# Side work of a two-layer trunk kernel: slices used in fours, B0/E0 in another tile, and the S5 tap matrices loaded early in pieces of 16 partitions

## The reference

```
x = x_prompt   (and again for x_sample, which reads cached context and starts from a given state)
for l in 0, 1:
    sh_m, sc_m, g_m, sh_f, sc_f, g_f = split(silu(c) @ ada_w[l] + ada_b[l], 6)          # "adaLN parts"
    h = x * (1 + sc_m) + sh_m
    out = [windowed attention | latent attention](h)     if l == 0
    out = s5_mixer(h)                                     if l == 1
    x = layer_norm(alpha * x + g_m * out)
    h = x * (1 + sc_f) + sh_f
    x = layer_norm(alpha * x + g_f * moe(h))              # 64 experts, top 6, and a shared one

s5_mixer: u = h @ w_in_c
          y = C (scan of lam_bar * state + b_bar u), forward and backward, + d * u
          z = gelu(y) @ w_out_c;  result z_val * sigmoid(z_gate)
moe:      sum over experts of gate_e * (silu(t @ w_gate_e) * (t @ w_up_e)) @ w_down_e
```

## Time and profile before

| what | value |
|---|---|
| median of three runs | 1595.81 us |
| the profiled execution | 1592.51 us |
| its span | 1590.7 us (1.8 us lie around it) |
| TensorE matmul busy | 1424.2 us, 90% of the span |
| VectorE busy | 1042.0 us, 66% |
| ScalarE busy | 582.7 us, 37% |
| DMA, mean over the span | 234 GB/s |

### The profile page before, as it was taken

The page is one execution under the profiler, slowest core; times in us unless marked ns, Lnnn a source line. Parts: engine busy times, 40 slices in busy tenths (PEclk is TensorE's granted clock), DMA queues, the critical chain, the costliest instruction groups (busy, mean ns, idle before and its releaser), DMA issues. The chain is left out here.

```text
span 1590.7 us, 26708 instructions
## 1 busy us (share of the span) xinstructions
PE 1424.2 (90%) x10938; PEld 1299.7 (82%) x10938; DVE 1042.0 (66%) x1542; ACT 582.7 (37%) x680; POOL 35.1 (2%) x37
## 2 busy tenths in 40 slices
PE   4887699999999999999955559599999999999996
PEld 1866688989988899899955559499999999999995
DVE  7534487788778888788861543866555655655655
ACT  2434253333333333333321553443343333333332
POOL 2000100000000000000020000100000000000001
PEclk8979889999999999999968779799999999999998
DMA  9763388999999888887767585265556555555530
GB/s 364 281 224 110 142 282 288 326 335 330 316 323 330 335 290 276 300 277 247 258 208 190 143 299 212 74 231 213 195 192 213 198 191 214 201 188 212 203 141 27
DMA packets 144688, 372.96 MB, mean 234 GB/s; under 512 B 16760, under 2 KB 63192, under 8 KB 141600
## 3 DMA queue, kind: packets, MB, share of 16 engines
q1 hardware_dynamic: 144608, 371.87, 68.2%
HBM read 349.21 MB, written 21.50 MB: 233 GB/s over the span
## 5 line engine op out<-in xcount | busy, mean ns | idle before, releaser
L271 PE MATMUL PS<-moe_mod_HThl,moe_up_h 128*128 128x256 f32 x2080 | 592.5, 285 | 2.3 <-DVE moe_up_l L1613 2.3
L272 PE MATMUL PS<-moe_mod_HThl,moe_up_h 128*128 128x256 f32 x2080 | 589.3, 283 | 0.0
L273 PE MATMUL PS<-moe_mod_HThl,moe_up_l 128*128 128x256 f32 x2080 | 589.2, 283 | 0.0
L271 PEld LDWEIGHTS PS<-moe_mod_HThl,moe_up_h 128*128 128x128 f32 x2080 | 399.3, 192 | 16.2 <-issue 9.4
L272 PEld LDWEIGHTS PS<-moe_mod_HThl,moe_up_h 128*128 128x128 f32 x2080 | 399.5, 192 | 3.6
L273 PEld LDWEIGHTS PS<-moe_mod_HThl,moe_up_l 128*128 128x128 f32 x2080 | 399.6, 192 | 0.0
L1613 DVE TENSOR_TENSOR moe_up_l<-raw,moe_up_h 128x2048 fp32r<-128x2048 f32 x130 | 297.2, 2287 | 36.0 <-ACT moe_up_h L1602 35.9
L1618 DVE TENSOR_TENSOR moe_down_l<-raw,moe_down_h 128x1024 fp32r<-128x1024 f32 x130 | 159.3, 1225 | 176.6 <-ACT moe_down_h L1606 176.6
L1602 ACT ACTIVATE moe_up_h<-raw 128x2048 fp32r<-128x2048 f32 x130 | 246.8, 1900 | 4.7 <-DMA raw<-in_exp_w_down 4.7
L1606 ACT ACTIVATE moe_down_h<-raw 128x1024 fp32r<-128x1024 f32 x130 | 137.7, 1059 | 294.7 <-PE PS L273 294.7
L271 PE MATMUL PS<-moe_down_h,moe_hid_h 128*128 128x512 f32 x520 | 204.1, 392 | 0.0
(11 more groups left out here) (384 smaller groups left out, 1419.6 us busy)
## 6 DMA issues: line engine op xcount, KB each, us to landing
raw<-in_exp_w_gate SPq DMA_DIRECT2D x128, 512.0 KB, 4.2
raw<-in_exp_w_up SPq DMA_DIRECT2D x128, 512.0 KB, 5.1
raw<-in_exp_w_down SPq DMA_DIRECT2D x128, 512.0 KB, 6.4
side_slices<-in_ada_w SPq DMA_DIRECT2D x56, 512.0 KB, 9.3
moe_gate_b<-gate_rows SPq DMA_DIRECT2D x128, 128.0 KB, 3.3
part_slices<-in_ada_w SPq DMA_DIRECT2D x18, 512.0 KB, 7.2
raw<-in_ada_w SPq DMA_DIRECT2D x8, 1024.0 KB, 10.9
s_from_state<-G SPq DMA_DIRECT2D x16, 512.0 KB, 4.4
```

What stands on the lines that cost most here:

```text
L271: pe.matmul(out, ah, bh, start=start, stop=False, skip_group_check=True)
L272: pe.matmul(out, ah, bl, start=False, stop=False, skip_group_check=True)
L273: return pe.matmul(out, al, bh, start=False, stop=stop, skip_group_check=True)
```

## The change

Six things change.

1. `used_at` puts four slices, not two, at one item in the first four groups: x = 3 and x = 7 (x = 3 and x = 6 in the fourth). The later three groups stay as they were. The second two slices of each four are loaded one step later than the rule "five steps after the slice before was used" gives (`late`).
2. The columns of a part are read back one step after its store, not two.
3. `E_ITEMS` has its doubled items at 10, 14, 18 and 26, not 11, 15, 19 and 27.
4. `B0` and `E0` move from `spare` into `G` at 2560, where the first place of `ET` is. So the load of `B0` waits until all 32 pieces are stored, and stands, with the second `load_f`, at step 36; before they stood at steps 33 and 35.
5. The taps are kept and stored in forward order, not reversed. The flips in the copy out and in the matmul's view go away.
6. `inside` is issued in pieces of 16 partitions. Eight transfers bring q = 0, 1, 2 together (16 partitions of 3 x 8 KB each), ahead of all loads of the into-state table but its tail; eight more bring q = 3, where it stood.

```diff
             def used_at(self, m):
                 n, y = divmod(m, SIDE)
+                if n < TAPS_GROUP - 1:
+                    return FIRST + SIDE * n + (3 if y < RING else 7)
+                if n == TAPS_GROUP - 1:
+                    return FIRST + SIDE * n + (3 if y < RING else 6)
                 return FIRST + SIDE * n + y // 2 * 2
...
                 for m in range(RING, N_SIDE * SIDE):
-                    if self.used_at(m - RING) + 5 == i:
+                    late = 1 if m - RING < TAPS_GROUP * SIDE and m % RING >= 2 else 0
+                    if self.used_at(m - RING) + 5 + late == i:
                         sp.wait_ge(part_used, SIDE * W_SIDE + m - RING + 1)
                         self.load(sp, m)
...
-                if 0 <= n < N_SIDE and step == (2 if n < N_SIDE - 1 else 1):
+                if 0 <= n < N_SIDE and step == 1:
                     sp.wait_ge(part_stored, 32 * (w + 1))
...
-            E_ITEMS = sorted(list(range(3, 31)) + [11, 15, 19, 27])
+            E_ITEMS = sorted(list(range(3, 31)) + [10, 14, 18, 26])
...
-                self.B0, self.E0 = spare[:, 1536:1792], spare[:, 1792:2048]
+                self.B0, self.E0 = at(2560, 256), at(2816, 256)
...
-                if i == self.FIRST_F + 2:
+                if done == self.FIRST_F:
+                    for b in range(3):
+                        sp.wait_ge(self.e_stored[b], 16 * ((34 - b) // 3))
                     self.load_b(sp, 0)
-                if i == self.FIRST_F + 4:
-                    sp.wait_ge(self.e_stored[1], 16 * 11)
                     self.load_f(sp, 1)
...
-                dve.tensor_copy(self.taps[:, :, m, :], PS[:, 3, 0:P].rearrange("p (s c) -> p s c", s=CH)[:, ::-1, :]).then_inc(self.k_out, 1)
+                dve.tensor_copy(self.taps[:, :, m, :], PS[:, 3, 0:P].rearrange("p (s c) -> p s c", s=CH)).then_inc(self.k_out, 1)
...
-                    return home.rearrange("p (s a c) -> p s a c", s=CH, a=NAT)[:, ::-1, a, :]
+                    return home.rearrange("p (s a c) -> p s a c", s=CH, a=NAT)[:, :, a, :]
...
-                        def inside(q):
-                            home = V[:, :] if q == 3 else MF[:, 2048 * q:2048 * q + 2048]
-                            tap = NAT * C5
-                            windows = bass.AP(kt_d.tensor, q * 15 * tap, [[tap, CH], [4 * 15 * tap, C5], [1, CH * tap]])
-                            sp.dma_start(home, windows).then_inc(m_landed[q // 3], 16)
+                        def inside(n, q):
+                            home = V if n else MF
+                            for s in range(CH):
+                                sp.dma_start(home[s * C5:(s + 1) * C5, :].rearrange("c (q x) -> c q x", x=2048),
+                                             kt_d[:, q, CH - 1 - s:2 * CH - 1 - s, :].rearrange("c q s x -> c q (s x)")).then_inc(m_landed[n], 16)
+                        inside(0, slice(0, 3))
                         into(0)
                         into(1)
                         rows(0)
                         into(2)
                         rows(1)
-                        for q in range(3):
-                            inside(q)
                         into(3)
                         rows(2)
                         rows(3)
                         sp.wait_ge(z_mm, 8)
-                        inside(3)
+                        inside(1, slice(3, 4))
...
-                                    pe.wait_ge(m_landed[q // 3], 16 if q else 48)
+                                    pe.wait_ge(m_landed[q // 3], 16 * CH)
```

More of the change, by code:

```diff
@@ L1438, in finish @@
                 for q in range(4):
-                    sp.dma_start(self.KT[32 * q:32 * q + C5, :], self.taps[32 * q + C5:32 * q + 2 * C5, 0, :, :]).then_inc(self.kt_landed, 16)
+                    sp.dma_start(self.KT[32 * q:32 * q + C5, :], self.taps[32 * q + C5:32 * q + 2 * C5, CH - 1, :, :]).then_inc(self.kt_landed, 16)
                 sp.wait_ge(self.kt_done, 1)
@@ L1442, in finish @@
                 for q in range(4):
-                    sp.dma_start(kt_d[:, q, 0:CH, :], taps[32 * q:32 * q + C5, :, :]).then_inc(self.kt_stored, 16)
-                    sp.dma_start(kt_d[:, q, CH:2 * CH - 1, :], taps[32 * q + C5:32 * q + 2 * C5, 1:CH, :]).then_inc(self.kt_stored, 16)
+                    sp.dma_start(kt_d[:, q, CH - 1:2 * CH - 1, :], taps[32 * q:32 * q + C5, :, :]).then_inc(self.kt_stored, 16)
+                    sp.dma_start(kt_d[:, q, 0:CH - 1, :], taps[32 * q + C5:32 * q + 2 * C5, 0:CH - 1, :]).then_inc(self.kt_stored, 16)
                 sp.wait_ge(self.kt_stored, 128)
@@ L1455, in gpsimd @@
                 pool.wait_ge(self.kt_step, 1)
-                centre = self.taps[:, CH - 1, :, :]
+                centre = self.taps[:, 0, :, :]
                 pool.tensor_tensor(centre, centre, self.KT.rearrange("p (a c) -> p a c", c=C5), ALU.add).then_inc(self.kt_done, 1)
```

## The result

The changed kernel takes 1611.71 us, the median of four runs (1609.88 to 1615.49), against 1595.91 for before: ratio 1.0107, 95% interval 1.0084 to 1.013. It is slower by 15.8 us; the forecast was 7.9. The profiled execution of after has a span of 1610.6 us, that of before 1590.7.

What follows compares the result with a forecast made beforehand. PE and the DMA queue were taken to bind together in MoE 0. Terms -2.6 - 3.6 + 9.1 + 3.5 + 3.5 - 2.0 = +7.9 on 1595.8 gave 1603.7 us, range 1587 to 1613.

Steps and rivals of the forecast that it cites:

- C: MoE 0: late slices have two items of lead, so PE waits at items 26 and 30; +9.1 us (0 to 16).
- E: Start of layer 1: early pieces delay the first chunk but free the last chunks' rows; +3.5 us (-8.1 to +12.9).
- A: MoE 0: eight mergers of two-slice blocks save 0.32 us of PE each; -2.6 us (0 to -3.8).
- B: MoE 0, item 28: the wait for the power rows and the half clock after it go away; -3.6 us.
- SP not late at step 28: MoE 0: stated sign of being wrong; the forecast had SP 9.6 us between gate and issue there.
- D: MoE 0: the late B0 load makes DVE wait 5 us and PE start item 34 late; +3.5 us (0 to +7).
- X: Layer 1: time the early pieces, 3.15 MB, occupy the queue ahead of the first chunk's rows; taken as 20 us.
- R4: Layer 1 rival: pieces crawl at 107 GB/s, delaying the first rows 29.4 us; total 1613.1 us, chance 0.12.
- The row of the stores: Evidence for layer 1's pieces: stores of taps, also 16 partitions each, moved 164 GB/s, which gives 19.2 us.
- F: Layer 1's out projection: ScalarE's 6.6 us wait for w_out_c shortens; -2.0 us (0 to -3.2).
- whether two items of lead suffice: MoE 0 rival: the shorter lead of late slices costs nothing; 1594.6 us, chance 0.21.
- a lateness under 4 us: MoE 0: SP's lateness below which two items of lead suffice, from a full lead of 18.3 us against landing 14.

Runs made afterwards that it cites:

- E0: Not a run but a buffer: in the changed kernel it moves with B0 from the spare tile into G; no time of its own.
- a2: The changed kernel with all four slices of a group loaded five steps after their slot's last use, a lead of three items; 1612.49 us.
- m2: The kernel before with slices in fours and no later step, plus doubled items and columns as changed; 1593.57 us.
- d_b0_alone: The kernel before with only B0 and E0 moved into G and their first load at step 36; 1604.76 us.
- c2: The kernel before with q = 0, 1, 2 loaded early as 24 transfers of 16 partitions x 8 KB, strips changing in turn; one execution, 1596.77 us.
- b1: The kernel before with only layer 1's tap matrices in pieces of 16 partitions, issued ahead of the into-state loads; layer 1 lost 7.1 us.
- b2: The kernel before with the tap matrices in pieces of 16 partitions at their old place, behind the rows of chunk 1; gained 4.1 us in layer 1.
- b5: The kernel before with the tap matrices in pieces of 16 partitions behind the rows of chunk 3; into-state products 15.7 us sooner, 12.5 given back.
- c1: The kernel before with eight pieces spread: two ahead of the rows of chunk 2, three ahead of chunk 3's, three behind; 1589.47 us.
- best2: m2 with 24 pieces, strips in turn, ten ahead of the rows of chunk 2 and fourteen ahead of chunk 3's; 1581.43 us.
- a1_pairs: The changed kernel with slices used and loaded in pairs at every second item as before the change; 1614.11 us.
- m1_fours: The kernel before with slices used in fours in the first four groups, no later step, B0 where it was; 1596.32 us.

## Why the prediction was wrong

The direction and the range held; the size was half. Two terms of the sum were too small, C (the short lead) and E (the start of layer 1). In the ledger of the changed kernel, blocks of slices counted at 1.19 and 2.05 us, the terms come out as follows.

- A, the mergers: -2.6 forecast. Two blocks of four in the changed kernel are 36.06 us apart (268.28, 304.34) where before it is 36.39: 0.33 for each merger, 0.32 forecast. Right.
- B, the wait at item 28: -3.6 forecast, some -4.5 measured (items 26 to 30, where kernels with the code of before differ by -0.6 to +1.4). Right in the changed kernel, for the second reason that was given: the waits of C give the queue time. Where these are taken away (a2, m2) the wait for the power rows comes back, at item 27, and PE waits 2.7 and 4.5 us.
- C, the short lead: this step failed. The prediction took SP's lateness from the trace of before and said of the earlier late pairs that "SP is not so late", so that only items 26 and 30 would wait. In the changed kernel item 18 waits with all it brings for 2.6 us, item 22 for 6.7, item 30 for 4.5, and 26 not at all: 13.8 for 9.1. The size of a stop does not give its price: item 18 stood for 2.1 us at full clock, item 22 for 3.6 and item 30 for 1.9 with a stretch at half clock behind each. The cause is in the change: pairs that had been loaded at every second step are now loaded in two neighbouring ones, 2 MB beside 3 MB of weights, and SP is 7.2 and 8.6 us late at the steps of items 18 and 22 where it was 3.2 and 4.9. At that of item 26, which was to wait most, the stops ahead had brought it down to 1.0 where it was 9.6, which is the prediction's own sign of being wrong (SP not late at step 28). I had the queue of before carry the order of after. By a2, taking the short lead away saves 9.7 us up to item 32, B's return included.
- D, `B0`: +3.5 forecast, 2.3 to 2.7 in the changed kernel, and VectorE's wait is the 5 us that was forecast. Near here, but by some luck: the waits of C, which the sum did not bring into this term, had shortened the queue. Its price alone is 8.1 (d_b0_alone), and after a2's smoother run 10.8; the prediction had this term's upper end at 7.
- E, the start of layer 1: +3.5 forecast, 9.1 measured. The mechanism and its sum were right, X - 16.5 and all; X was mis-sized, 25.1 for 20, because the pieces' 129 to 137 GB/s are nearer to the windows' 139 than to the 164 of the stores of taps. R4's total, 1613.1, is the nearest to 1611.71, but by luck: its X of 29.4 is 4.3 too long, and it has the 9.1 of C, 4.7 too little. The row of the stores misled me: there, as in c2, each transfer has one packet for each engine and the strip changes with each transfer, where the early pieces have three in one strip; they also read SBUF and do not write it. The Trainium skill, "SBUF — State Buffer", section "Door 1: The DMA port swizzle (why [64,N] ≈ [32,N])", gives 104 GB/s for a transfer over partitions 0 to 15 and would have put X at an estimated 30; the trace has 129 to 137 GB/s and 25.1, between that and my 20. c2, at 209 to 213 GB/s, fits its rule that the partitions of a transfer limit the rate, and shows that taking strips in turn gets round it. What the Trainium skill, "DMA: Bandwidth & Descriptors", section "Why a DMA increments its semaphore by 16 and not by 1", says, that the number of engines is the largest one up to 16 that divides the slowest dimensions of both sides, agrees with the shares (1.02 for the pieces against 45.3% for the windows). But twice the engines brought no more GB/s here (134 against 139).
- F, `w_out_c`: -2.0 forecast; 7.4 at the end against 9.1 at the last chunk is -1.7, and ScalarE's wait for `w_out_c` is 4.2 us where it was 6.6. Right.

The errors of C (4.7) and E (5.6), less B and D, make the 8.5 us between the forecast sum and the 16.4 of the traces.

The rivals' question in MoE 0, whether two items of lead suffice, was put rightly; its deciding point, a lateness under 4 us, also: in the changed kernel the short leads with SP 3.0 and 1.0 us late (items 14 and 26) suffice, and those with 7.2, 8.6 and 6.7 (items 18, 22, 30) do not. I read the lateness from the wrong kernel.

## What to carry to other kernels

Where a queue is full, work out how late the issuer is from the new order of issues and not from the old trace: bunching the same bytes into neighbouring steps made a lead of two items too short. Costs that come from one full queue do not add: here 6.4 us with the late slices alone (one trace, and no more than the noise of MoE 0) and 8.1 of a late table made 9.0 together, so taking out either alone gained almost nothing, and each must be tested alone on the kernel before. A large load belongs in a gap that the timeline shows, cut so that neighbouring transfers write to different partitions.

## What the hardware showed

- Transfers of 16 partitions x 24 KB with all engines busy ran at 129 to 137 GB/s in the changed kernel and at 119 to 152 in the windows of 4 us of b1, b2 and b5; the same bytes as 16 x 8 KB with the strip changing each time at 209 to 213 (c2).
- With the engines full of the slow packets PE stopped for 9.7 us within a run of matmuls whose data was there, released by nothing in the profile (b5); with the pieces spread or in turn (c1, c2, best2) it did not.
- An overlapping-window source over 128 partitions was worse than pieces, by 12.3 us early and 8.9 last (4.1 at the old place, near the noise), though at the old place its packets left half of the engines' time unused (45.3%).
- The same late load of 128 KB held VectorE for 5.3 (changed kernel), 8.7 (d_b0_alone), 9.3 (a1_pairs) and 11.2 us (a2_no_late); it was the shortest where PE had last waited closest ahead of it, at item 30.
- A stop of PE of 1.9 us was followed by a granted clock of 0.50 (item 30 of the changed kernel, and the earlier trace rows); one of 2.1 us at item 18 and one of 3.4 us in m1_fours were not.
